# 1/rms of the recurrence's rows made by GpSimd with a power instead of ScalarE's root and VectorE's reciprocal

## The reference, cut to what matters

```python
def step(carry, inp):                       # per chunk
    C, n, m = carry
    ...
    s = jnp.einsum('bhtd,bhsd->bhts', q_, k_) * dexp
    num = jnp.einsum('bhts,bhsd->bhtd', s, v_) + inter_w[..., None] * jnp.einsum('bhtd,bhde->bhte', q_, C)
    den = jnp.sum(s, axis=-1) + inter_w * jnp.einsum('bhtd,bhd->bht', q_, n)
    h = num / jnp.maximum(jnp.abs(den), jnp.exp(-m_t))[..., None]
    ...
    C_new = decay[..., None, None] * C + jnp.einsum('bhs,bhsd,bhse->bhde', ws, k_, v_)

y_a = rmsnorm_2(h, mh_norm_g...) * jax.nn.sigmoid(o)      # y = x * rsqrt(mean(x*x) + 1e-6) * g
return (g_a * y_a + g_b * y_b) @ w_out
```

## Time and profile before

| | us |
|---|---|
| median of 3 runs | 2496.06 (2493.95 to 2497.55) |
| the profiled execution | 2496.99 |
| its span, first to last instruction | 2495.2 |
| TensorE busy | 2420.6 (97%) |
| VectorE busy | 1306.2 (52%) |
| ScalarE busy | 1111.1 (45%) |
| GpSimd busy | 592.6 (24%) |

### The profile page before, as it was taken

How to read it: one execution, slowest core, us unless ns; L and a number is a source line. 1 busy time by engine, 2 the same in 40 slices (tenths; PEclk the granted TensorE clock), 3 DMA queues, 4 the chain that set the end, 5 groups by cost and what they waited for, 6 DMA issues and landing times. The chain is left out here.

```text
span 2495.2 us, 31548 instructions
## 1 busy us (share of the span) xinstructions
PE 2420.6 (97%) x12674; PEld 2007.0 (80%) x12674; DVE 1306.2 (52%) x1642; ACT 1111.1 (45%) x1604; POOL 592.6 (24%) x488
## 2 busy tenths in 40 slices
PE   8999999999999999999999898999999999999997
PEld 7888888667877788888888787877888888888885
DVE  5755011385512221213644285335269999898985
ACT  5610221485333121212422274232237787878783
POOL 0121231230321131223322066224111114311100
PEclk9999999999999999999999999999999999999999
DMA  7822321342231113123232474222558999999996
GB/s 285 301 88 82 110 76 51 89 130 100 93 118 35 34 51 135 35 76 115 90 110 68 154 279 159 85 76 62 194 197 365 378 388 387 397 387 384 375 375 243
DMA packets 138298, 446.45 MB, mean 179 GB/s; under 512 B 20952, under 2 KB 63640, under 8 KB 121512
## 3 DMA queue, kind: packets, MB, share of 16 engines
q1 hardware_dynamic: 95728, 378.14, 40.4%
q0 software_dynamic: 16208, 38.39, 4.2%
q10 hardware_dynamic: 26216, 27.89, 3.5%
HBM read 385.06 MB, written 77.14 MB: 185 GB/s over the span
## 5 line engine op out<-in xcount | busy, mean ns | idle before, releaser
L3215 DVE TENSOR_TENSOR ex_w_lo<-ex_w,ex_w_hi 128x2048 fp32r<-128x2048 f32 x198 | 447.8, 2290 | 53.1 <-ACT ex_w_hi L3151 51.7
L3151 ACT ACTIVATE ex_w_hi<-ex_w 128x2048 fp32r<-128x2048 f32 x198 | 377.0, 1916 | 24.3 <-PE ex_pb L3081 9.9
L249 POOL TENSOR_TENSOR p_w_lo<-w_raw,p_w_hi 128x512 fp32r<-128x512 f32 (+1 forms) x138 | 181.0, 1342 | 594.5 <-ACT p_w_hi L275 593.7
L316 PE MATMUL p_ps<-hT_hi,p_w_hi 128*128 128x512 f32 (+1 forms) x608 | 219.0, 360 | 3.3 <-DVE p_w_lo L249 3.1
L318 PE MATMUL p_ps<-hT_hi,p_w_lo 128*128 128x512 f32 (+1 forms) x608 | 217.6, 358 | 0.0
L317 PE MATMUL p_ps<-hT_lo,p_w_hi 128*128 128x512 f32 (+1 forms) x608 | 217.6, 358 | 0.0
L275 ACT ACTIVATE p_w_hi<-w_raw 128x512 fp32r<-128x512 f32 (+1 forms) x200 | 112.4, 607 | 213.1 <-PE p_ps L318 88.1
L249 POOL TENSOR_TENSOR p_w_lo_rest<-w_raw,p_w_hi_rest 128x512 fp32r<-128x512 f32 x64 | 86.8, 1385 | 207.1 <-ACT p_w_hi_rest L275 207.1
L316 PEld LDWEIGHTS p_ps<-hT_hi,p_w_hi 128*128 128x128 f32 x608 | 116.3, 191 | 21.0 <-DVE hT_lo L712 3.4
L318 PEld LDWEIGHTS p_ps<-hT_hi,p_w_lo 128*128 128x128 f32 x608 | 116.2, 191 | 16.4
L317 PEld LDWEIGHTS p_ps<-hT_lo,p_w_hi 128*128 128x128 f32 x608 | 116.2, 191 | 15.8
(11 more groups left out here) (537 smaller groups left out, 6029.5 us busy)
## 6 DMA issues: line engine op xcount, KB each, us to landing
ex_w<-w SPq DMA_DIRECT2D x99, 2048.0 KB, 14.3
w_raw<-w_in SPq DMA_DIRECT2D x36, 1024.0 KB, 5.3
w_raw<-w_xkv_panels SPq DMA_DIRECT2D x8, 1024.0 KB, 6.0
w_raw<-w_out SPq DMA_DIRECT2D x8, 1024.0 KB, 9.2
x_rows<-o_x SPq DMA_DIRECT2D x16, 512.0 KB, 2.6
qk_columns<-ml_qk_first ACTq DMA_DIRECT2D x16, 512.0 KB, 3.2
w_raw<-w_qk_panels SPq DMA_DIRECT2D x6, 1024.0 KB, 7.6
w_raw<-w_xo_panels SPq DMA_DIRECT2D x4, 1024.0 KB, 5.4
```

The lines of the kernel that those rows point to most:

```text
L249: emit(self.lo(n)[:, 0:w], self.half(n // (KC // 2), w)[:, n % (KC // 2), :], self.hi(n)[:, 0:w].bitcast(F32), ALU.subtract).then_inc(self ...
L316: pe.matmul(out, a, x, start=start, stop=False)
L3151: nc.scalar.activation(w_hi[:, n % RING, :], raw_half(n), ACT.Copy).then_inc(hi_done, 1)
L3215: nc.vector.tensor_tensor(w_lo[:, n % RING, :], raw_half(n), w_hi[:, n % RING, :].bitcast(F32), ALU.subtract).then_inc(down_lo if m == "w2 ...
```

## The change

1/rms of a chunk's four heads is made by GpSimd: mean plus epsilon by one TENSOR_SCALAR, then a TENSOR_TENSOR with the power -0.5, whose exponents lie in a new tile `root` of four columns. The first stands behind a wait for the last square of the chunk (`rms_ready`, now raised by that square), the second behind a wait for the first. `invert_rms(t)` stands at the head of GpSimd's chunk t, so behind the weight pieces of chunk t - 1, and in chunk 7 ahead of its last two pieces. ScalarE has no root and VectorE no reciprocal of it any more. The first square of a chunk waits for `rstd_ready` where it waited for `rms_ready`, and `keep_mixed` follows the squares.

GpSimd clears the state, and VectorE waits for that ahead of its first state. VectorE raises `start` after the ones in the values. ScalarE runs an exponential of one column right after `start`, which brings the exponential's table. In the last chunk VectorE's low part is written ahead of the queries, which that chunk hasn't.

```diff
+        root = s.enter_context(nc.sbuf_tensor("ml_root", [P, MH], F32))
...
             @block.gpsimd
             def _(pool):
+                def invert_rms(t):
+                    pool.wait_ge(rms_ready, t + 1)
+                    c.gstep(pool, nc.gpsimd.tensor_scalar(ss[:, 1, :], ss[:, 0, :], 1.0 / MD, EPS, ALU.mult, ALU.add))
+                    if t >= 1:
+                        pool.wait_ge(rows_scaled, t)
+                    nc.gpsimd.tensor_tensor(ss[:, 2, :], ss[:, 1, :], root[:, :], ALU.pow).then_inc(rstd_ready, 1)
+
                 ready = 0
+                nc.gpsimd.memset(root[:, :], -0.5).then_inc(cleared, 1)
+                nc.gpsimd.memset(st[:, :, :, :], 0.0).then_inc(cleared, 1)
...
+                pool.wait_ge(cleared, 2)
                 for t in range(NT):
+                    invert_rms(t)
                     if t + 1 < NT:
...
                     dve.wait_ge(c_done, u + 1)
+                    if u == 0:
+                        dve.wait_ge(cleared, 2)
...
-                def invert_rms(t):
-                    dve.wait_ge(rms_ready, t + 1)
-                    if t >= 1:
-                        dve.wait_ge(rows_scaled, t)
-                    nc.vector.reciprocal(ss[:, 2, :], ss[:, 1, :]).then_inc(rstd_ready, 1)
...
+                nc.vector.tensor_scalar(never[:, :], c.const("causal"), 1.0, -NEVER, ALU.subtract, ALU.mult)
                 nc.vector.memset(eps[:, :], EPS)
                 for b in range(2):
-                    nc.vector.memset(v[b][:, :, MD:MV], 1.0)
-                nc.vector.tensor_scalar(never[:, :], c.const("causal"), 1.0, -NEVER, ALU.subtract, ALU.mult)
-                nc.vector.memset(st[:, :, :, :], 0.0).then_inc(start, 1)
+                    ins = nc.vector.memset(v[b][:, :, MD:MV], 1.0)
+                ins.then_inc(start, 1)
...
                     if t + 1 < NT:
                         gaps(t + 1)
-                        scale_queries(t + 1)
                     if t == NT - 1:
                         dve.wait_ge(out.first_hi, 1)
                         out_low(0, out.first_lo)
-                    if t >= 1:
-                        invert_rms(t - 1)
+                    if t + 1 < NT:
+                        scale_queries(t + 1)
...
                 out_low(1, out.rest)
-                invert_rms(NT - 1)
...
                 act.wait_ge(start, 1)
+                c.astep(act, nc.scalar.activation(ss[:, 0, 0:1], eps[:, :], ACT.Exp))
                 exps(0)
...
                         if h == 0 and t >= 1:
-                            act.wait_ge(rms_ready, t)
-                        c.astep(act, nc.scalar.activation(sq[:, :], hh[:, t % 2, h * MD:(h + 1) * MD], ACT.Square,
-                                                          accum_out=ss[:, 0, h:h + 1]))
-                        if h == MH - 1 and t >= 1:
-                            keep_mixed(t - 1)
+                            act.wait_ge(rstd_ready, t)
+                        ins = nc.scalar.activation(sq[:, :], hh[:, t % 2, h * MD:(h + 1) * MD], ACT.Square,
+                                                   accum_out=ss[:, 0, h:h + 1])
+                        if h < MH - 1:
+                            c.astep(act, ins)
+                    ins.then_inc(rms_ready, 1)
                     if t >= 1:
-                        act.wait_ge(rstd_ready, t)
-                    nc.scalar.activation(ss[:, 1, :], ss[:, 0, :], ACT.Sqrt, scale=1.0 / MD, bias=eps[:, :]
-                                         ).then_inc(rms_ready, 1)
+                        keep_mixed(t - 1)
```

More of the change, by code:

```diff
@@ L1939, in mlstm @@
         og_in, yb_in = [c.sem(f"ml_og_in{b}") for b in range(2)], c.sem("ml_yb_in")
-        start = c.sem("ml_start")
+        start, cleared = c.sem("ml_start"), c.sem("ml_cleared")
         s_done, k_turned = c.sem("ml_s_done"), c.sem("ml_k_turned")
```

## The result

Before 2495.35 us and after 2509.51 us, medians of four runs each: ratio 1.0052, 95% interval 1.0040 to 1.0064. The changed kernel is slower by about 14 us. Measured again later it was 1.0056 (1.0039 to 1.0072). The profiled execution took 2509.19 us with a span of 2507.4, which is 12.2 us more than before by either measure.

The account below looks back on a forecast made before the run. The prediction took a loop through VectorE, ScalarE, GpSimd and TensorE to set the recurrence's pace. Opening -0.1, chunks -3.7, end +2.8 and next table load +0.05 gave about -1.0 us: median 2495.1 us, range 2491 to 2502.

Parts of the forecast that it names:

- The ring: In each recurrence chunk: VectorE's reciprocal, ScalarE's scaling, GpSimd's two operations, TensorE's transposes, VectorE's state and queries set the 13.62 us period.
- the two places of the account: Between the chunks' multiplications the change would gain 3.7 us; at the end of the stage it would lose 2.8 us.
- the formula for GpSimd's loop: In one chunk GpSimd's own queue takes 11.95 us plus T, forecast at 12.75 us.
- T: In each chunk, from the end of GpSimd's weight instructions to ScalarE's scaling: taken as 0.8 us, range 0.5 to 1.85.
- four transitions: Between GpSimd's multiplications in the chunks: four at 12.8 instead of 13.62 us, together 3.2 us gained.
- dear power: Rival, GpSimd's power in the chunks and at the end: T up to 1.85, then +5.8 us, 2501.8 us; chance 0.18.
- The port: Rival, GpSimd's power beside VectorE's queries in the chunks: they exclude each other, total +3.8 us, 2499.8 us; chance 0.20.
- The end: In the last chunks: +2.1 us before chunk 6's multiplication, +0.7 before the last weights, together +2.8 us.
- The opening: At the recurrence's start: first weighing nearly 3 us sooner, but chunk 1's scores wait for their DMA, so 0.1 us gained.
- The tables: ScalarE's table loads: none left in the stage, the next block's root needs one of 1.28 us, just covered, +0.05 us.
- Dear: over 1 us with VectorE idle: Sign in the profile that GpSimd's power is itself expensive: it lasts over 1 us while VectorE is idle.
- Port: ends behind the queries: Sign in the chunks' profile that VectorE holds GpSimd off: the power lasts over 1 us or ends just behind VectorE's queries.

Follow-up runs that it names:

- the repeat: The changed kernel as it is, measured again with no further change: ratio to the kernel before 1.0056 (1.0039 to 1.0072), block 132.03 us.
- the run with 32 products: The changed kernel plus 32 unused identity products on TensorE ahead of its last wait for weights: ratio to the kernel before 1.0062, block 133.43 us.

## Why the prediction was wrong, step by step

**What bounds: right.** The ring, the two places of the account (chunks and end) and the formula for GpSimd's loop, 11.95 + T, were right: with the measured T of 2.48 to 2.50 it gives 14.43 to 14.45 us, and 14.48 was measured. The gain I had forecast for the chunks, 3.7 us, is nearly that of the kernel whose inverse stands between the pieces (3.6), but that is partly luck: I had four transitions at 12.8 us and a first one that gains only 0.5, and all five ran at 12.90.

**The step that failed is the size of T**, the time from the end of the weights to the scaling. I took 0.8 us; it was 2.49. The TENSOR_SCALAR (0.20) was right. The power was taken at 0.3 as "nearest to the 245 ns row". That row was near in size, but the operation was another; a power of four columns is 1.03 us, five times a multiplication of the same tile. My upper bound, the 1.27 us of 512 columns, held it. With 1.03 alone T is 1.44, as in chunk 6. My chances don't fit that bound either: two thirds of "dear power" lay beyond 5 us, which by my formula needs T over 1.75, while I let T reach 1.85 at most.

**The second failure is that I made rivals of two things that add up.** "The port" was priced with a cheap power, "the power is dear" without the port, so neither case nor the upper end of T at 1.85 could give 2.50. The port's rival was right in its mechanism, its partner, its start (I said 1493.47 and 1493.45; here 1494.13 and 1494.16) and in who waits, for which I had no row. With both, my own formulas would have said: five chunk transitions from 13.62 to 14.45, +4.2; chunk 6 with T = 1.44, 1.44 + 1.78 - 0.47 = +2.75; chunk 7, +1.3. That is 8.2 of the 10.9 us, and slower by over 0.2%.

**The end: place right, size too small.** I had +2.1 and +0.7. Measured were +2.8 and +2.4 (the last weight piece). The first is T again. In the second, 1.3 is the inverse, and 1.1 is the multiplication for chunk 6, which came to lie on VectorE's second low part (3.49 instead of 2.36): a move on GpSimd's queue changed whom it met, which I had not looked for. I forecast that TensorE would wait 3 to 4 us for the last L249; it waited 3.88. But I let the delay count one to one. Behind it came 2.0 us in the block and 1.6 in the next at half clock (1.4 in all in the repeat), a term that the sum had at nothing. A row with the price of half clock stood in my own groups: the 16 scores of 3.64 us behind a pause of 3.57, against 1.95 elsewhere; the granted clock of the first was 0.53.

**The opening: right in its sum, half wrong in its working.** The scores were bound by the landing as said, at 1422.69 and so 5.9 us into the block; I had 6.3 (1424.5 - 1418.2), so 0.5 came and not 0.1; with a landing that gave 5.66 to 6.69 in ten profiles, no forecast to a tenth could hold. That GpSimd's clearing costs nothing was wrong: VectorE's mask, 0.23 us before, took 1.89 beside it. So the first weighing gained 1.8 us instead of nearly 3. It didn't matter, since it was not the last to arrive.

**The tables: right.** No table load is left in the chunks, and the next block's load is just hidden, as I had it: 0.06 us of slack in the repeat, and 0.05 to 0.13 in five other profiles without the root that had TensorE at full clock behind the block (1.73 in the first profile, at half clock). In the run with 32 products ScalarE came about 1.1 us later there and TensorE waited 0.93 us for the rows, so nothing is left in reserve. No draining was seen behind it: the root starts at 1558.48, 0.01 us after the load's end. By the page of the Trainium skill that I had weighed (ScalarE: Activation LUTs, What ACT_TABLE_LOAD costs) there would be about 1.38 us more; the trace doesn't show them.

**The rest.** +2.7 us lie behind the block, of which 1.6 are the clock, read at the next block's transposes. The other 1.1, and the 1.4 that the part ahead of the block was shorter, are within what executions of these kernels show without a cause in the change: the stretch behind the block lasted 955.3 us before, 958.1 and 954.8 in the two profiles of the changed kernel and 952.4 to 960.9 over all runs. I leave them open. The signs to look for were well chosen, "Dear: over 1 us with VectorE idle" and "Port: ends behind the queries" among them: both came true at once.

## What to carry to other kernels

Price an operation by its kind first and by its size second; where no row has the kind, take the range's upper end into the forecast once it stands on a loop that sets the pace. Add up rivals that share an instruction, before giving them chances. An operation put on another engine's queue costs by its place: the same power at the head of the chunk made the kernel 0.5% slower, and one weight piece earlier, with the end relieved, 0.2% faster than before.

## What the runs showed of the hardware

- On GpSimd a TENSOR_TENSOR with the power on 128x4 took 1.01 to 1.05 us alone, the same instruction with a multiplication 0.20. VectorE's two-input queries, begun 0.53 us into that 1.03, ran undelayed (1.21), while either GpSimd operation, begun 0.02 to 0.03 us behind them, took 1.05 us longer. That it is the reading of SBUF that meets, and not the computing, fits these rows; no run shows it by itself.
- A one-input TENSOR_SCALAR of VectorE (128x128) took 1.89 us beside GpSimd's memset of 1.81 us, and 0.23 without it.
- TensorE's granted clock fell from 1.00 to 0.50, its 1.2 GHz level, around waits of 3.88 us (low at once) and 3.47 us (low 1.0 us later), and once with no pause over 1.94 us in that stage's end. It stayed low for 10.2 us in one execution of the changed kernel and for 3.4 in another. With 3.73 us of unneeded products in the wait it stayed high.
- Filling TensorE's pause for the clock's sake gained 4.3 us of the time here, but products that last longer than the wait cost more than they save (133.43 against 132.49 us for the block, with 32; 130.45 with 16).
